# Keeping the attention queries and keys in fp32: one fp32 score matmul in place of three fp32r ones

## The chip, the cores and the metric

The kernel runs on one core of a Trainium2 chip. The metric is the device time of one execution in microseconds, the median over runs. The reference computes in fp32, and the kernel follows it on TensorE in two ways: a tensor is split into a rounded part and a remainder, both of type fp32r, and a product is three fp32r matmuls (high by high, high by low, low by high); or, in a few small places, an unsplit fp32 matmul is issued.

## The reference, cut to what matters

Three transformer blocks on a sequence of 512 positions of width 1024. The parts that the change touches are the scores of three attentions, all with head dimension 64:

```
# differential attention, 4 heads, 2 maps each
sc = einsum('bhmqd,bhmkd->bhmqk', q, k) * scale - slope * dist
p = softmax(sc);  w = p[:, :, 0] - lam * p[:, :, 1];  o = w @ v
# bidirectional retention, 4 heads: (q k^T * decay) @ v
# banded attention, 16 query heads, 4 key heads, blocks of 128, window 128
scores = einsum('bcqhgd,bckhd->bchgqk', rope(q), rope(k)) * hd ** -0.5
```

Around them stand input projections, gates, output projections, an mLSTM mixer and two feed-forward layers; they are the bulk of the matmuls.

## The kernel before

Activations lie feature-major in SBUF as eight tiles of 128x512 (XH and XL are the split, normed input). Weights stream in chunks of 1 MB into RAW (two buffers) and are split by ScalarE and VectorE into WH and WL. `mm3` (line 234) issues the three fp32r matmuls of a product; `mm` (line 226) issues one matmul of whatever type its operands have. `split` (line 247) is the pair of instructions that makes high and low parts: a copy on ScalarE (line 202), then a subtraction on VectorE (line 215).

Split activations live in FR, a pool of 25 buffers of 128x512 (`NFR`, `fr.take`, `fr.put`); unsplit ones in FT, a pool of 12. PSUM has eight banks (`bank`).

The order of the work on each engine is fixed when the program is built. Two Python generators, a main one (projections, then the output projection) and a side one (the heads), are interleaved by `weave` (line 122): each queue carries a planned time, each token a planned due time, and whichever stream is due is emitted next, the side one first when both are. A generator that yields None is blocked until the other one moves. At run time every engine follows its own list in order and waits on the others by semaphores.

Three stages matter here:

- **Block 1.** `block1_proj` projects; before each q chunk (queries and keys of one differential head) and each r chunk (retention) it waits until `len(fr.q) >= 4 + 2 * held[0]`. `qk_norm3` and the r branch split their results into FR. `diff_heads` computes the scores of 16 items (4 heads x 4 query tiles), each item two maps: map 0 contracts over partitions 0 to 63, map 1 over 64 to 127. `ret_heads` does 16 items with one score product each.
- **Banded attention.** `a_proj` projects keys (chunk 0), values (chunk 1), and queries (chunks 2 to 5, called pairs 0 to 3), with the same FR test before each q or k chunk; `rope2` rotates each of the ten tiles, with an fp32 matmul against a permutation, and splits it into FR. `a_heads` works through 32 items (pair, query block, half); stage 1 of an item is two score products over the same 64 partitions, 384 columns wide for inner query blocks and 256 wide for the first and last. Later stages do the softmax, transpose the weights, split them into FR and multiply with the values. It keeps 8 FR buffers for itself; the keys hold 4 and every query pair 4, which come free when the pair's last item is done.
- **Output projection.** `out_proj` splits each finished mixed tile into two FR buffers (`make`, `parts`), which it keeps to its end, as soon as the tile is there and FR has room. Its matmuls read FR and WH, WL.

Of the kernel before, what the change touches and what calls it, by code (L numbers as in the profile page):

```python
# [5 lines left out]
ALU = mybir.AluOpType  # L6
# [150 lines left out]
def blocks_kernel(nc, A, out):  # L157
# [16 lines left out]
    SM = sb("SM", [128, NSMALL])  # L174
    G = sb("G", [128, KT, S])
    VV = sb("VV", [128, 4 * 4 * 258], F32R)
    FR = sb("FR", [128, NFR, S], F32R)
    FT = sb("FT", [128, NFT, S])
    STR = sb("STR", [128, 896])
    ONE = sb("ONE", [128, 128])  # L180
# [53 lines left out]
    def mm3(o, L, R, start, stop, *after, last=None):  # L234

        mm(o, L[0], R[0], start, False, *after, last=False)
        mm(o, L[0], R[1], False, False, last=False)
        return mm(o, L[1], R[0], False, stop, last=last)

    def tr(o, i, ident, *after, last=True):  # L240
        f = lambda e: e.transpose(o, i, ident)  # L241
# [236 lines left out]
    def block1_proj():  # L478
        for c in B_ORDER:
            n = int(c[1])  # L480
            if c[0] == "a":
                yield from vproj("va", n)
                if n == 1:
                    small1()
                    strips()
            elif c[0] == "v":
                yield from vproj("vr", n)
            elif c[0] == "q":
                while len(fr.q) < 4 + 2 * held[0]:
                    yield None  # L490
                j, h, l, wt = w_use()
                for u in range(2):
                    yield from fm_tile(h, l, wt, u * 128)
                    b, t = st["pb"], st["pt"]
                    got = qk_norm1(b, t)
                    held[0] += 1
                    soon.append((got[3], lambda n=n, u=u, got=got: qk_step2(n, u, got)))
                w_done[j] = t
            elif c[0] == "g":
                j, h, l, wt = w_use()  # L500
                for u in range(2):
                    yield from fm_tile(h, l, wt, u * 128)
                    gate_tile(st["pb"], st["pt"], 2 * n + u, ACT.Silu)
                w_done[j] = st["pt"]
            else:
                while len(fr.q) < 4 + 2 * held[0]:
                    yield None
                j, h, l, wt = w_use()
                for u in range(2):
                    fh, f1 = fr.take()  # L510
                    fl, f2 = fr.take()
                    yield from fm_tile(h, l, wt, u * 128)
                    b, t = st["pb"], st["pt"]
                    f, ff = ft.take()
                    t1 = stt(FT[:, f, :], PS[:, b, :], 1.0 if n == 0 else 0.125, RB[:, :], ALU.mult, ALU.mult, t, st["rbt"], ff)
                    bank.put(b, t1)
                    st["rb_read"] = t1
                    tk = split(FT[:, f, :], FR[:, fh, :], FR[:, fl, :], t1, f1, f2)
                    ft.put(f, tk)
                    ready["rqk", n, u] = (fh, fl, tk)  # L520
                w_done[j] = t
        while held[0]:
            yield None
        st["xfree"] = st["pt"]
# [79 lines left out]
    def qk_norm3(x):  # L604
        f, t1, n, t, wcol = x
        b, fb = bank.take()
        t = spread(b, lambda i: FT[:, n, i * 128:(i + 1) * 128], t, fb)
        ft.put(n, t)
        w = ready["w8"][0] if wcol == C_QN else SM[:, wcol:wcol + 1]
        t = stt(FT[:, f, :], FT[:, f, :], w, PS[:, b, :], ALU.mult, ALU.mult, t, t1, ready["w8"][1], t_sm)  # L610
        bank.put(b, t)
        fh, f1 = fr.take()
        fl, f2 = fr.take()
        tk = split(FT[:, f, :], FR[:, fh, :], FR[:, fl, :], t, f1, f2)
        ft.put(f, tk)
        return fh, fl, tk

    def small1():

# [67 lines left out]
    def diff_heads():  # L687
# [10 lines left out]

        def scores(hd, qt, tb):

            (qh, ql, qt_), (kh, kl, kt_) = ready["qk", hd]
            r = []
            for m in range(2):
                b, fb = bank.take()
                p = slice(64 * m, 64 * m + 64)
                q = (FR[p, qh, qt * 128:(qt + 1) * 128], FR[p, ql, qt * 128:(qt + 1) * 128])
                t = mm3(PS[:, b, :], q, (FR[p, kh, :], FR[p, kl, :]), True, True, qt_, kt_, fb)
                st["qk_read"] = t
                s, sf = ft.take()
                nm, sm, rs = sc(), sc(), sc()  # L710
                bs = STR[:, 384 - 128 * qt:896 - 128 * qt]
                t1 = DV.op(lambda e, s=s, b=b, bs=bs, nm=nm: e.tensor_tensor_reduce(
                    out=FT[:, s, :], in0=PS[:, b, :], in1=bs, scale=1.0, scalar=-NEG,
                    op0=ALU.add, op1=ALU.min, accum_out=nm), t, tb, sf, us=0.6)
                bank.put(b, t1)
                r.append((s, sm, nm, t1, rs))
                st["bias_read"] = t1
            return r
# [25 lines left out]
        def values(hd):  # L744
            b, fb = bank.take()
            for kt in range(4):
                cc = slice(hd * 128, hd * 128 + 128)
                t = mm3(PS[:, b, :], (VT[:, 0, kt, cc], VT[:, 1, kt, cc]),
                        (FR[:, w0:w0 + 4, kt * 128:kt * 128 + 128], FR[:, w0 + 4:w0 + 8, kt * 128:kt * 128 + 128]),
                        kt == 0, kt == 3, wtok[hd], ready["va", hd // 2], fb)  # L750
            wfree[0] = ready["dpv", hd] = t
            for x in ready["qk", hd]:
                fr.put(x[0], st["qk_last", hd])
                fr.put(x[1], st["qk_last", hd])
            if hd == 3:
                for i in range(8):
                    fr.put(w0 + i, t)
            return head_norm(b, t, hd, ready["sub"])

        s1, s2 = {}, {}  # L760
        for n in range(len(items) + 3):
            if n < len(items):
                hd, qt = items[n]
                while ("qk", hd) not in ready:
                    yield None
                if qt == 0:
                    tb = bias(hd)
                yield [ready["qk", hd][0][2], ready["qk", hd][1][2]]
                s1[n] = scores(hd, qt, tb)
                if qt == 3:  # L770
                    st["qk_last", hd] = st["qk_read"]
# [55 lines left out]
    def ret_heads():  # L827
# [6 lines left out]
        for n in range(len(items) + 3):  # L834

            st["fr_kept"] = 8 - 2 * len(got) if n < len(items) else 0
            if n < len(items):
                hd, kt = items[n]
                u, p = hd // 2, slice(64 * (hd % 2), 64 * (hd % 2) + 64)
                qh, ql, qt_ = ready["rqk", 0, u]  # L840
                kh, kl, kt_ = ready["rqk", 1, u]
                if kt == 0:
                    tb = ts(STV, dp, lg[:, hd:hd + 1], ALU.mult, td, tlg, st.get("bias_read"))
                    tb = stt(STV, dn, lg[:, 4 + hd:5 + hd], STV, ALU.mult, ALU.add, tb, tlg)
# [1 line left out]
                yield [qt_, kt_]  # L846
                b, fb = bank.take()
                c = slice(kt * 128, kt * 128 + 128)
                t = mm3(PS[:, b, :], (FR[p, kh, c], FR[p, kl, c]), (FR[p, qh, :], FR[p, ql, :]), True, True, qt_, kt_, fb)
                f, ff = ft.take()  # L850
                t1 = tt(FT[:, f, :], PS[:, b, :], STR[:, 384 - 128 * kt:896 - 128 * kt], ALU.mult, t, tb, ff)
                st["bias_read"] = t1
# [5 lines left out]
                got[n] = (gh, gl, tk)  # L858
                st["fr_kept"] -= 2
                if hd % 2 and kt == 3:  # L860
                    for x in (qh, ql, kh, kl):
                        fr.put(x, t)
            k = n - 3
            if k >= 0:
# [487 lines left out]
    def rope2(x):  # L1352
# [5 lines left out]
        ta = tt(FT[:, g, :], PS[:, b, :], FT[:, si, :], ALU.mult, t2, tr_, gf)  # L1358
        bank.put(b, ta)
        tb = tt(FT[:, f, :], FT[:, f, :], FT[:, ci, :], ALU.mult, t2, tr_, t1)  # L1360
        tb = tt(FT[:, f, :], FT[:, f, :], FT[:, g, :], ALU.add, ta, tb)
        ft.put(g, tb)
        fh, f1 = fr.take()
        fl, f2 = fr.take()
        tk = split(FT[:, f, :], FR[:, fh, :], FR[:, fl, :], tb, f1, f2)
        ft.put(f, tk)
        st["rope_read"] = [ta, tb]
        return fh, fl, tk

    def a_proj():  # L1370
        V = VV[:, 0:4096].rearrange("p (a i k d) -> p a i k d", a=2, i=4, k=4)
# [59 lines left out]
    def a_heads():  # L1431
# [6 lines left out]
        def stage1(n):  # L1438
# [4 lines left out]
            W = (k1 - k0) * 128  # L1443
            mo = K_BAND + (128 if qb == 0 else 0)
            mask = CO[:, mo:mo + W]
            kh, kl, tk_ = ready["ak",][m]
            p = slice(64 * ab, 64 * ab + 64)
            hq = (2 * m + ab) * 4 + (pr % 2) * 2
            mx, nm, es, sm, dn, rd = [sc(2) for _ in range(6)]
            S_, t1 = [], []  # L1450
            for g in range(2):
                qh, ql, tq = ready["aq", pr][g]
                b, fb = bank.take()
                qq = slice(qb * 128, qb * 128 + 128)
                t = mm3(PS[:, b, 0:W], (FR[p, qh, qq], FR[p, ql, qq]),
                        (FR[p, kh, k0 * 128:k1 * 128], FR[p, kl, k0 * 128:k1 * 128]), True, True, tq, tk_, fb)
                s, sf = ft.take()
                o_, i_, a_ = FT[:, s, 0:W], PS[:, b, 0:W], mx[:, g:g + 1]
                x = DV.op(lambda e, o_=o_, i_=i_, a_=a_: e.tensor_tensor_reduce(  # L1459
# [35 lines left out]
        def stage4(n, ptok, W):  # L1495
# [19 lines left out]
            if qb == 3:  # L1515
                for g in range(2):
                    ready["mix", 2 * pr + g] = ready["mixl", 2 * pr + g]
                for y in ready["aq", pr]:
                    fr.put(y[0], st["aq_last", pr])
                    fr.put(y[1], st["aq_last", pr])  # L1520
            st["apv"] = t

        s1, s2, s3 = {}, {}, {}
        for n in range(len(items) + 3):
            if n < len(items):
                while ("aq", items[n][0]) not in ready or "av" not in ready:
                    yield None
                yield [y[2] for y in ready["aq", items[n][0]] + ready["ak",]]
                s1[n] = stage1(n)
            if n - 1 in s1:  # L1530
                s2[n - 1] = stage2(*s1.pop(n - 1))
# [7 lines left out]
            fr.put(p0 + i, st["apv"])  # L1539
        for x in ready["ak",]:  # L1540
            fr.put(x[0], st["apv"])
            fr.put(x[1], st["apv"])
        ci, si, _ = ready["rope"]
        ft.put(ci, st["rope_read"])
        ft.put(si, st["rope_read"])
# [168 lines left out]
```

How the kernel before makes its waits and increments, by code:

```python
    def play(self, eng, sems):  # L90
        for need, fn, inc in self.items:
            for k, v in need:
                eng.wait_ge(sems[k], v)
            ins = fn(eng)
            if inc:
                ins.then_inc(sems[inc[0]], inc[1])
# [1488 lines left out]
        @block.sync  # L1585
        def _(e):
            SP.play(e, sems)
            e.wait_ge(sems["out"], 16 * KT)
```

## Time and profile before

| | |
|---|---|
| median of 3 runs | 1562.91 us (1561.32 to 1566.44) |
| span of the profiled execution | 1564.8 us |
| TensorE busy | 1482.5 us, 95% |
| VectorE, ScalarE busy | 886.6 us, 57%; 597.9 us, 38% |
| mean granted TensorE clock | 0.974 |

The span runs from the first to the last instruction. No time of its own is listed for the profiled execution beside the three runs; its span lies 1.9 us above their median and 1.6 us below their highest. Times in the rows are microseconds from the start of the span; durations of a single instruction, where a column says so, are nanoseconds. PE is TensorE, DVE is VectorE, ACT is ScalarE. Matmuls are pipelined: one that is shown as 0.39 us long lets the next start 0.23 us after it.

### The profile page before, as it was taken

To read this page: it belongs to the slowest core of one execution; us is meant where nothing else is said; L and a number is where in the kernel's file an instruction comes from. 1 tells how busy PE (TensorE), PEld (TensorE's weight loads), DVE (VectorE), ACT (ScalarE), POOL (GpSimd) and SP (SyncE) were. 2 spreads that over 40 slices of the span, in tenths; PEclk is the share of its full clock that TensorE was granted. 3 is DMA by queue.
4 is the path that set the end of the run, shared out by engine and by line. 5 is a ranking of instruction groups with operands and counts; after the bars stand their busy time and mean duration, and the time that the engine had idled before them with its cause. 6 is when DMAs were issued, how large, how long until landed. Compare 5 with 4: busy or idle time off the path is not lost.

```text
span 1564.8 us, 18661 instructions
## 1 busy us (share of the span) xinstructions
PE 1482.5 (95%) x7280; PEld 1227.6 (78%) x7280; DVE 886.6 (57%) x1712; ACT 597.9 (38%) x1078; POOL 37.8 (2%) x43
## 2 busy tenths in 40 slices
PE   7999998998999689999999999988989999999997
PEld 7777785787888568888888878776768888888885
DVE  5677856666676664443344466687755544344433
ACT  5555533454444443222233233455544322222321
POOL 0011000000000000000000000000000000000000
PEclk9999997999999899999999999989999999999998
DMA  6122110131221113312322233200002222323221
GB/s 226 58 80 81 48 62 27 41 108 54 81 76 45 43 54 108 108 64 96 123 97 93 74 108 108 81 27 18 11 28 96 93 101 78 107 105 108 69 91 69
DMA packets 20903, 123.07 MB, mean 79 GB/s; under 512 B 2256, under 2 KB 2896, under 8 KB 9680
## 3 DMA queue, kind: packets, MB, share of 16 engines
q1 hardware_dynamic: 20816, 121.89, 22.6%
q8 instruction: 58, 0.95, 0.2%
q14 instruction: 29, 0.24, 0.1%
HBM read 119.78 MB, written 2.10 MB: 78 GB/s over the span
## 4 chain that ended last, share of the span: by engine, by line
PE 42%; issue 24%; DVE 7%; ACT 3%; DVEq 0%; POOLq 0%; POOL 0%; ACTq 0%
PE PS L227 41%; DVE FT L223 2%; PE PS L241 1%; DVE FR L215 1%; ACT FR L202 1%; ACT WH L202 1%; DVE WL L215 1%; ACT FT L202 1%; DVE FT L219 1%; DVE FT L215 0%; DVE SC L220 0%; DVE FT L1459 0%; DVE G L215 0%; ACT XH L202 0%; DVE XT L215 0%
## 5 line engine op out<-in xcount | busy, mean ns | idle before, releaser
L227 PE MATMUL PS<-XH,WH 128*128 128x512 f32 x1080 | 427.2, 396 | 0.0
L227 PE MATMUL PS<-XH,WL 128*128 128x512 f32 x1080 | 420.8, 390 | 0.0
L227 PE MATMUL PS<-XL,WH 128*128 128x512 f32 x1080 | 420.6, 389 | 0.0
L227 PE MATMUL PS<-FR,WH 128*128 128x512 f32 x1088 | 345.7, 399 | 18.9 <-DVE FR L215 13.2
L215 DVE TENSOR_TENSOR WL<-RAW,WH 128x1024 fp32r<-128x1024 f32 (+2 forms) x242 | 263.2, 1129 | 137.9 <-ACT WH L202 136.9
L202 ACT ACTIVATE WH<-RAW 128x1024 fp32r<-128x1024 f32 (+2 forms) x242 | 223.8, 974 | 144.0 <-PE PS L227 137.8
L227 PEld LDWEIGHTS PS<-FR,WH 128*128 128x128 f32 x1088 | 205.3, 192 | 68.7 <-issue 8.1
L227 PEld LDWEIGHTS PS<-XH,WH 128*128 128x128 f32 x1080 | 202.8, 188 | 46.8 <-issue 6.2
L227 PEld LDWEIGHTS PS<-XH,WL 128*128 128x128 f32 x1080 | 202.7, 188 | 42.8
L227 PEld LDWEIGHTS PS<-XL,WH 128*128 128x128 f32 x1080 | 202.9, 188 | 40.8 <-issue 0.7
L227 PE MATMUL PS<-FR,WL 128*128 128x512 f32 x544 | 215.3, 396 | 0.0
L202 ACT ACTIVATE FR<-FT 128x512 fp32r<-128x512 f32 (+3 forms) x118 | 69.4, 588 | 355.2 <-DVE FT L215 296.9
L215 DVE TENSOR_TENSOR FT<-PS,RB 128x512 f32<-128x512 f32 x89 | 61.0, 688 | 213.8 <-PE PS L227 200.8
L215 DVE TENSOR_TENSOR FR<-FT,FR 128x512 fp32r<-128x512 f32 (+3 forms) x118 | 75.3, 638 | 85.4 <-ACT FR L202 85.4
L227 PEld LDWEIGHTS PS<-FR,WL 128*128 128x128 f32 x544 | 104.2, 192 | 22.2
L227 PE MATMUL PS<-WH,XH 128*128 128x256 f32 x288 | 84.1, 292 | 11.4 <-DVE XL L223 11.4
L227 PE MATMUL PS<-FR 64*128 64x512 f32 (+3 forms) x384 | 85.0, 391 | 7.3 <-DVE G L215 2.9
L202 ACT ACTIVATE FT<-FT 128x512 f32<-128x512 f32 (+2 forms) x81 | 40.7, 504 | 125.0 <-DVE FT L215 100.9
L227 PE MATMUL PS<-WL,XH 128*128 128x256 f32 x288 | 82.5, 286 | 0.0
L227 PE MATMUL PS<-WH,XL 128*128 128x256 f32 x288 | 82.4, 286 | 0.0
L227 PEld LDWEIGHTS PS<-FR 64*128 64x128 f32 (+1 forms) x384 | 57.0, 200 | 30.8 <-issue 14.6
L227 PE MATMUL PS<-FR,VV 128*128 128x256 f32 (+1 forms) x336 | 65.2, 335 | 12.0 <-DVE FR L215 11.8
(110 smaller groups left out, 1331.0 us busy)
## 6 DMA issues: line engine op xcount, KB each, us to landing
RAW<-in_f_in SPq DMA_DIRECT2D x44, 1024.0 KB, 4.9
RAW<-in_w_in SPq DMA_DIRECT2D x13, 1024.0 KB, 4.9
RAW<-in_m_in SPq DMA_DIRECT2D x12, 1024.0 KB, 4.9
RAW<-in_f_oa SPq DMA_DIRECT2D x16, 768.0 KB, 4.2
RAW<-in_f_ob SPq DMA_DIRECT2D x16, 640.0 KB, 3.9
RAW<-in_a_in SPq DMA_DIRECT2D x6, 1024.0 KB, 4.9
RAW<-in_w_out SPq DMA_DIRECT2D x4, 1024.0 KB, 4.9
RAW<-in_m_out SPq DMA_DIRECT2D x4, 1024.0 KB, 4.9
```

The source lines that it names most:

```text
L202: return AC.op(lambda e: e.activation(o, i, f, scale=scale) if accum is None else e.activation(o, i, f, scale=scale, accum_out=accum), *af ...
L215: return q.op(lambda e: e.tensor_tensor(o, a, b, op), *after, us=us)
L219: return q.op(lambda e: e.tensor_scalar(o, a, s1, None, op0), *after, us=dve_us(o))
L223: return DV.op(lambda e: e.scalar_tensor_tensor(out=o, in0=a, scalar=s, in1=b, op0=op0, op1=op1), *after, us=dve_us(o))
L227: f = lambda e: e.matmul(o, l, r, start=start, stop=stop, skip_group_check=True)
L241: f = lambda e: e.transpose(o, i, ident)
```

## The change

Query and key tiles of the three attentions are no longer split. They are written once, in fp32, into FP, a second view of the memory of FR with type fp32, so that each takes one buffer of the pool and not two. Their scores are one fp32 matmul each (`mm4`), and the planner is told that it lasts as long as two fp32r matmuls of that width. All waits that asked for the split's end now ask for the one VectorE instruction that writes the tile. The FR tests ahead of the chunks stay as they are.

```diff
-    FR = sb("FR", [128, NFR, S], F32R)
+    at, _ = nc.bump_sbuf(NFR * S * 4)
+    FR = nc.alloc_sbuf_tensor_at("FR", [128, NFR, S], F32R, offset=at)
+    FP = nc.alloc_sbuf_tensor_at("FP", [128, NFR, S], F32, offset=at)
...
+    def mm4(o, l, r, start, stop, *after, last=None):
+        f = lambda e: e.matmul(o, l, r, start=start, stop=stop, skip_group_check=True)
+        us = 2 * 0.00042 * width(o)
+        if stop if last is None else last:
+            return PE.op(f, *after, us=us)
+        PE.quiet(f, *after, us=us)
+        return None
...
# block1_proj, r branch (qk_norm3 likewise)
-                    t1 = stt(FT[:, f, :], PS[:, b, :], 1.0 if n == 0 else 0.125, RB[:, :], ALU.mult, ALU.mult, t, st["rbt"], ff)
+                    t1 = stt(FP[:, f, :], PS[:, b, :], 1.0 if n == 0 else 0.125, RB[:, :], ALU.mult, ALU.mult, t, st["rbt"], ff)
-                    tk = split(FT[:, f, :], FR[:, fh, :], FR[:, fl, :], t1, f1, f2)
-                    ft.put(f, tk)
-                    ready["rqk", n, u] = (fh, fl, tk)
+                    ready["rqk", n, u] = (f, t1)
...
# rope2
-        tb = tt(FT[:, f, :], FT[:, f, :], FT[:, g, :], ALU.add, ta, tb)
+        x, xf = fr.take()
+        tb = tt(FP[:, x, :], FT[:, f, :], FT[:, g, :], ALU.add, ta, tb, xf)
-        fh, f1 = fr.take()
-        fl, f2 = fr.take()
-        tk = split(FT[:, f, :], FR[:, fh, :], FR[:, fl, :], tb, f1, f2)
...
# diff_heads; ret_heads and a_heads likewise
-                t = mm3(PS[:, b, :], q, (FR[p, kh, :], FR[p, kl, :]), True, True, qt_, kt_, fb)
+                t = mm4(PS[:, b, :], FP[p, q, qt * 128:(qt + 1) * 128], FP[p, k, :], True, True, qt_, kt_, fb)
```

## Rows read from the trace of the kernel before

**Rows 1.** The page: span, and busy time of each engine.

```profile
span 1564.8 us, 18661 instructions
...
PE 1482.5 (95%) x7280; PEld 1227.6 (78%) x7280; DVE 886.6 (57%) x1712; ACT 597.9 (38%) x1078; POOL 37.8 (2%) x43
```

**Rows 2.** Busy time in stretches (columns: length, PE, PEld, DVE, ACT, POOL, clock, DMA).

```profile
40.00:214.00 174.00, 170.66 (x916) 137.97 (x915) 123.98 (x286) 91.39 (x159) 17.11 (x12) 1.00 0.19 67
214.00:290.00 76.00, 69.54 (x324) 51.32 (x322) 46.10 (x70) 26.06 (x41) 5.15 (x4) 0.89 0.08 28
...
1026.00:1050.00 24.00, 19.76 (x101) 16.85 (x99) 19.27 (x67) 12.56 (x44) 0.00 (x0) 0.72 0.12 44
1050.00:1080.00 30.00, 30.00 (x179) 25.07 (x178) 22.88 (x88) 15.48 (x54) 0.00 (x0) 1.00 0.00 1
1080.00:1154.00 74.00, 60.05 (x341) 48.78 (x339) 53.50 (x190) 39.13 (x128) 0.00 (x0) 0.90 0.05 15
```

**Rows 3.** The same columns, for three stretches at the lower clock.

```profile
238.50:255.50 17.00, 14.39 (x35) 9.45 (x35) 11.39 (x17) 7.66 (x12) 1.38 (x1) 0.50 0.18 62
1030.50:1044.00 13.50, 11.27 (x48) 9.79 (x46) 9.12 (x36) 6.87 (x24) 0.00 (x0) 0.50 0.14 60
1088.50:1102.00 13.50, 10.00 (x33) 7.82 (x32) 8.91 (x24) 5.37 (x16) 0.00 (x0) 0.50 0.23 79
```

**Rows 4.** Waits of TensorE between 1026 and 1154 us.

```profile
PE PS L227 <- DVE FR L215: 16.3, 11, 3.5
```

**Rows 5.** Timeline: the two longest of those waits (columns: start, length, instruction, wait).

```profile
1087.60 0.95 PE L227 MATMUL PS<-FR,VV 128*128 128x256 f32 x6 [2.79 <-DVE FR L215]
...
1092.86 1.19 PE L227 MATMUL PS<-FR,WH 128*128 128x512 f32 x2 [3.50 <-DVE FR L215]
```

**Rows 6.** Timeline: fp32r matmuls of 512 columns, back to back.

```profile
145.82 0.39 PE L227 MATMUL PS<-XH,WH 128*128 128x512 f32 x1
...
146.50 0.39 PE L227 MATMUL PS<-XH,WH 128*128 128x512 f32 x1
```

**Rows 7.** Timeline: one fp32 matmul of 512 columns (two records) amid fp32r ones.

```profile
965.03 1.02 PE L227 MATMUL PS<-FT,CO 128*128 128x512 f32 x2
...
965.50 0.68 PE L227 MATMUL PS<-WH,XH 128*128 128x256 f32 x1
...
966.01 0.28 PE L227 MATMUL PS<-WL,XH 128*128 128x256 f32 x1
```

**Rows 8.** Timeline: the scores of one differential item, and what follows.

```profile
144.12 0.97 PE L227 MATMUL PS<-FR 64*128 64x512 f32 x6
...
145.02 0.50 PE L227 MATMUL PS<-XH,WH 128*128 128x512 f32 x1
```

**Rows 9.** Timeline: the first retention scores, four items in a row.

```profile
214.29 3.01 PE L227 MATMUL PS<-FR 64*128 64x512 f32 x12
```

**Rows 10.** Timeline: one banded item of 384 and one of 256 columns, and their successors.

```profile
1052.98 1.31 PE L227 MATMUL PS<-FR 64*128 64x384 f32 x6
1054.23 0.50 PE L227 MATMUL PS<-XH,WH 128*128 128x512 f32 x1
...
1072.95 0.97 PE L227 MATMUL PS<-FR 64*128 64x256 f32 x6
1073.85 0.50 PE L227 MATMUL PS<-XH,WH 128*128 128x512 f32 x1
```

**Rows 11.** Groups by shape (count | busy us, mean ns of one | idle before, releaser).

```profile
L215 DVE TENSOR_TENSOR FR<-FT,FR 128x512 fp32r<-128x512 f32 x94 | 65.1, 692 | 72.2 <-ACT FR L202 72.2
...
L202 ACT ACTIVATE FR<-FT 128x512 fp32r<-128x512 f32 x94 | 59.4, 632 | 342.1 <-DVE FT L215 296.9 <-DVE FT L223 45.2
...
L227 PE MATMUL PS<-FR 64*128 64x512 f32 x144 | 31.3, 435 | 2.9 <-DVE G L215 2.9
...
L227 PE MATMUL PS<-FR 64*128 64x384 f32 x96 | 22.8, 371 | 0.2 <-DVE FR L215 0.2
...
L227 PE MATMUL PS<-FR 64*128 64x256 f32 x96 | 16.4, 314 | 0.0
```

More of the change, by code:

```diff
@@ L509, in block1_proj @@
                 for u in range(2):
-                    fh, f1 = fr.take()
-                    fl, f2 = fr.take()
+                    f, ff = fr.take()
                     yield from fm_tile(h, l, wt, u * 128)
                     b, t = st["pb"], st["pt"]
-                    f, ff = ft.take()
-                    t1 = stt(FT[:, f, :], PS[:, b, :], 1.0 if n == 0 else 0.125, RB[:, :], ALU.mult, ALU.mult, t, st["rbt"], ff)
+                    t1 = stt(FP[:, f, :], PS[:, b, :], 1.0 if n == 0 else 0.125, RB[:, :], ALU.mult, ALU.mult, t, st["rbt"], ff)
                     bank.put(b, t1)
                     st["rb_read"] = t1
-                    tk = split(FT[:, f, :], FR[:, fh, :], FR[:, fl, :], t1, f1, f2)
-                    ft.put(f, tk)
-                    ready["rqk", n, u] = (fh, fl, tk)
+                    ready["rqk", n, u] = (f, t1)
                 w_done[j] = t
@@ L609, in qk_norm3 @@
         w = ready["w8"][0] if wcol == C_QN else SM[:, wcol:wcol + 1]
-        t = stt(FT[:, f, :], FT[:, f, :], w, PS[:, b, :], ALU.mult, ALU.mult, t, t1, ready["w8"][1], t_sm)
+        x, xf = fr.take()
+        t = stt(FP[:, x, :], FT[:, f, :], w, PS[:, b, :], ALU.mult, ALU.mult, t, t1, ready["w8"][1], t_sm, xf)
         bank.put(b, t)
[L612 to L616, printed above, removed]
+        ft.put(f, t)
+        return x, t
     def small1():
@@ L699, in scores @@
         def scores(hd, qt, tb):
-            (qh, ql, qt_), (kh, kl, kt_) = ready["qk", hd]
+            (q, qt_), (k, kt_) = ready["qk", hd]
             r = []
@@ L705, in scores @@
                 p = slice(64 * m, 64 * m + 64)
-                q = (FR[p, qh, qt * 128:(qt + 1) * 128], FR[p, ql, qt * 128:(qt + 1) * 128])
-                t = mm3(PS[:, b, :], q, (FR[p, kh, :], FR[p, kl, :]), True, True, qt_, kt_, fb)
+                t = mm4(PS[:, b, :], FP[p, q, qt * 128:(qt + 1) * 128], FP[p, k, :], True, True, qt_, kt_, fb)
                 st["qk_read"] = t
@@ L753, in values @@
                 fr.put(x[0], st["qk_last", hd])
-                fr.put(x[1], st["qk_last", hd])
             if hd == 3:
@@ L767, in diff_heads @@
                     tb = bias(hd)
-                yield [ready["qk", hd][0][2], ready["qk", hd][1][2]]
+                yield [ready["qk", hd][0][1], ready["qk", hd][1][1]]
                 s1[n] = scores(hd, qt, tb)
@@ L839, in ret_heads @@
                 u, p = hd // 2, slice(64 * (hd % 2), 64 * (hd % 2) + 64)
-                qh, ql, qt_ = ready["rqk", 0, u]
-                kh, kl, kt_ = ready["rqk", 1, u]
+                q, qt_ = ready["rqk", 0, u]
+                ky, kt_ = ready["rqk", 1, u]
                 if kt == 0:
@@ L848, in ret_heads @@
                 c = slice(kt * 128, kt * 128 + 128)
-                t = mm3(PS[:, b, :], (FR[p, kh, c], FR[p, kl, c]), (FR[p, qh, :], FR[p, ql, :]), True, True, qt_, kt_, fb)
+                t = mm4(PS[:, b, :], FP[p, ky, c], FP[p, q, :], True, True, qt_, kt_, fb)
                 f, ff = ft.take()
@@ L860, in ret_heads @@
                 if hd % 2 and kt == 3:
-                    for x in (qh, ql, kh, kl):
+                    for x in (q, ky):
                         fr.put(x, t)
@@ L1360, in rope2 @@
         tb = tt(FT[:, f, :], FT[:, f, :], FT[:, ci, :], ALU.mult, t2, tr_, t1)
-        tb = tt(FT[:, f, :], FT[:, f, :], FT[:, g, :], ALU.add, ta, tb)
+        x, xf = fr.take()
+        tb = tt(FP[:, x, :], FT[:, f, :], FT[:, g, :], ALU.add, ta, tb, xf)
         ft.put(g, tb)
-        fh, f1 = fr.take()
-        fl, f2 = fr.take()
-        tk = split(FT[:, f, :], FR[:, fh, :], FR[:, fl, :], tb, f1, f2)
-        ft.put(f, tk)
+        ft.put(f, tb)
         st["rope_read"] = [ta, tb]
-        return fh, fl, tk
+        return x, tb
     def a_proj():
@@ L1445, in stage1 @@
             mask = CO[:, mo:mo + W]
-            kh, kl, tk_ = ready["ak",][m]
+            ky, tk_ = ready["ak",][m]
             p = slice(64 * ab, 64 * ab + 64)
@@ L1451, in stage1 @@
             for g in range(2):
-                qh, ql, tq = ready["aq", pr][g]
+                q, tq = ready["aq", pr][g]
                 b, fb = bank.take()
                 qq = slice(qb * 128, qb * 128 + 128)
-                t = mm3(PS[:, b, 0:W], (FR[p, qh, qq], FR[p, ql, qq]),
-                        (FR[p, kh, k0 * 128:k1 * 128], FR[p, kl, k0 * 128:k1 * 128]), True, True, tq, tk_, fb)
+                t = mm4(PS[:, b, 0:W], FP[p, q, qq], FP[p, ky, k0 * 128:k1 * 128], True, True, tq, tk_, fb)
                 s, sf = ft.take()
@@ L1519, in stage4 @@
                     fr.put(y[0], st["aq_last", pr])
-                    fr.put(y[1], st["aq_last", pr])
             st["apv"] = t
@@ L1527, in a_heads @@
                     yield None
-                yield [y[2] for y in ready["aq", items[n][0]] + ready["ak",]]
+                yield [y[1] for y in ready["aq", items[n][0]] + ready["ak",]]
                 s1[n] = stage1(n)
@@ L1541, in a_heads @@
             fr.put(x[0], st["apv"])
-            fr.put(x[1], st["apv"])
         ci, si, _ = ready["rope"]
```

## The prediction

> **What bounds the kernel now.** I read the page first: TensorE is busy 1482.5 of 1564.8 us, VectorE 57%, ScalarE 38% [rows 1]. So work added to TensorE costs about its own length wherever TensorE has no holes, and work taken from VectorE and ScalarE pays only through a hole that it closes. Next the busy time in stretches, to see where holes are. The differential stage (40 to 214 us) has 3.3 us of them in 174; the retention stage (214 to 290) has 6.5; the banded stage has 4.2 between 1026 and 1050, none in the next 30 us, and 14.0 between 1080 and 1154 [rows 2]. The granted clock is 1.00 in the dense stretches and 0.72, 0.89 and 0.90 where the holes are. Asking for the low stretches alone shows full half-clock stretches (0.50, that is 1.2 in place of 2.4 GHz), each beginning at or just after a hole: TensorE is busy 14.39, 11.27 and 10.00 us in them [rows 3]. At the full clock that work would take about half, so they cost some 7.2, 5.6 and 5.0 us on top of the holes themselves. Then the waits: from 1026 to 1154 the waits of TensorE are put down to VectorE's FR writes, 16.3 us [rows 4], the longest 2.79 and 3.50 us [rows 5].
>
> What starves TensorE there is read from the code beside these rows. With 25 FR buffers, a_heads holds 8, the keys 4, pairs 0, 1 and 2 hold 12: one is left, and the projection of pair 3 wants 4. It is blocked until pair 0 is done, and between 1026 and 1050 the heads run with nothing to fill their latency. The same happens to the output projection: its first two mixed tiles exist once pair 0 is done, but with all pairs projected only 25-8-4-12 = 1 buffer is free until pair 1 is done; its first matmul is the one that waits 3.50 us at 1092.86 [rows 5].
>
> **What the scores cost.** The steady fp32r matmul of 512 columns: from 145.82 to 146.50 lie three starts, 0.227 us each [rows 6], 0.68 per product. An fp32 product of 512 columns exists once in kind, the rotation matmul: two records, first at 965.03; the second record behind it (WL,XH) starts normally at 966.01, and its neighbour of 256 columns takes about 0.12 of array time, so the fp32 product holds the array from 965.03 to 965.89, 0.86 us [rows 7]. One fp32 matmul is thus 0.18 us dearer than the three it replaces, with all 128 rows.
>
> *Retention*: one product per item on one half of the rows. Twelve matmuls take 3.01 us including the last one's tail, so 64-row fp32r matmuls on the same rows follow each other at the same 0.23 [rows 9]. 16 items x 0.18 = +2.9 us.
>
> *Differential*: the six matmuls of an item last 0.97 us together, and the next stream starts 0.90 after the first of them [rows 8]; in series they would need 6 x 0.227 = 1.36. So the two maps, on different halves of the rows, run side by side: three slots of 0.227 plus 0.22 at the change of shape. If fp32 matmuls pair in the same way, an item takes 0.86 + 0.22 = 1.08, +0.18, and 16 items +2.9 us. If they do not, 2 x 0.86 + 0.22 = 1.94, +1.04, +16.6 us. No row shows an fp32 pair. I take the paired value, because nothing in the 64-row fp32r rows distinguishes the maps except their rows, which stay as they are, and keep the other for the range.
>
> Here a rule of the Trainium skill speaks against the rows: "TensorE: Matmul & The Clock Gate", Part 3 (The mechanism), says that matmuls start and end strictly in program order, and only weight loads are pulled ahead. The program order is three of map 0, then three of map 1, so by that rule just one adjacent couple overlaps, and the item would take five slots, not the three that [rows 8] show; the trace does not agree. Applied to the new item it gives three half-products of 0.43 in a row in place of two, which is the in-order rival below.
>
> *Banded*: both products of an item use the same rows, so nothing pairs. Six matmuls and their change of shape take 1.25 us at 384 columns and 0.90 at 256 [rows 10]; less 0.20 that is 1.05 and 0.70. The fp32 cost scaled by width is 2 x 0.86 x 384/512 = 1.29 and 2 x 0.86 x 256/512 = 0.86: +0.24 and +0.16. The 96 matmuls of either width are 16 items [rows 11]: 3.8 + 2.6 = +6.4 us. From below, if 64-row fp32 were no dearer than its planned two slots, each product would fall from three slots to two; from above, 0.18 per product whatever its width gives 64 x 0.18 = 11.5.
>
> Scores together: 2.9 + 2.9 + 6.4 = **+12.2 us**, all on TensorE.
>
> **What the splits give.** 22 splits go (8 differential tiles, 4 retention, 10 banded), each 0.632 us of ScalarE and 0.692 of VectorE [rows 11]: 13.9 and 15.2 us. The 12 of block 1 lie behind 3.3 us of holes in 174 and are worth nothing. The 10 banded ones shorten the rotation, which shares VectorE with the softmax; they act through the holes counted next. If that cover of TensorE work were absent, a tile would be ready 1.3 us sooner, ten times; 13 us is the most they could be worth.
>
> **What the buffers give.** Banded stage after: 8 + 2 + 4 x 2 = 18, seven left. The test for 4 passes for every pair, so the 16 products of pair 3 are there at 1026 to fill the heads' latency. I count the first shortage as gone: 4.2 us of holes and 5.6 of slow clock, -9.8. The second (holes of 2.79 and 3.50, slow clock 5.0, together 11.3) comes when pair 3 is projected and VectorE is loaded with its rotation and with weight splits; the FR room removes one of its causes, but now that moment comes earlier, when pair 0 has only just delivered tiles. I take half, -5.6. The drain of the last items, the remaining 7.7 us of holes before 1154, stays, as nothing is left to fill it. Block 1: differential heads follow their q chunks there and TensorE has no holes; in the retention stage out_proj begins when the values and its first weights are ready, not when FR has room. Nothing gained in either. No DMA is added or moved past another; the weight loads follow the chunks, and pair 3's chunk asks for its successor some 20 us sooner, with the queues nearly empty then (DMA share 0.12) [rows 2].
>
> Sum: 12.2 - 9.8 - 5.6 = **-3.2 us**, from 1564.8 to 1561.6 of span. No run is listed as the profiled one; what lies around the span is at most the 1.6 us to the highest run, and the edit does not touch it. Against the median of 1562.9 the same difference gives 1559.7; I forecast 1560.
>
> **The rivals.**
>
> *Both shortages vanish.* All of 9.8 + 11.3 = 21.1 against 12.2: -8.9, 1554. For it: between 1050 and 1080, with pair 3's products as filler, there is no hole at all [rows 2]. Against: the filler is only moved, and what pair 3 fills early it cannot fill late. Chance 0.22.
>
> *The gain is spent.* Filler used before 1050 is missing between 1050 and 1080, the hole and the slow clock move there, and only the score cost is left: +12.2, 1575. For it: the planner books an fp32 product at 0.43 us per 512 columns where I measure 0.86, so it believes TensorE free some 0.4 us per product too early and hands out filler too freely; VectorE is busy 53.5 of 74 us at the end [rows 2]. It decides once the moved hole exceeds about 7 us. Slower. Chance 0.20.
>
> *fp32 pairs do not overlap.* +16.6 in place of +2.9 in the differential stage: -3.2 + 13.7 = +10.5, 1573. Decides if more than about half of the overlap is lost. Chance 0.13.
>
> *In-order pairs.* Three half-products in series: +0.43 per item, 16 x 0.43 = 6.9 over the forecast: 1567. The trace so far speaks against it, chance 0.05.
>
> *The scores are cheaper than I count*, two slots per product as planned. Then differential and retention lose 0.23 per item, 7.4 us; banded 1.05 to 0.70 and 0.70 to 0.47, 16 x 0.58 = 9.3; with the 15.4 of buffers -32, 1531. Against it speak [rows 7]. Chance 0.04.
>
> **How the numbers follow.** The forecast has 0.36, its own range 1554 to 1567 (none or all of the second shortage). About 0.3% (4.7 us) is what a measurement of this kernel can tell from no change, so 1558.2 and 1567.6 are the borders. Faster: 0.12 of the forecast, 0.22, 0.04 = 0.38. Same: 0.24 of the forecast, 0.03 of the in-order pairs, 0.03 of the spent gain = 0.30. Slower: 0.17 + 0.13 + 0.02 = 0.32. The range reaches from beneath the second case to above the spent gain: 1547 to 1579.
>
> **What would show it.** Two score records per product in place of three; an fp32 product 0.86 us of array time at 512 columns; differential items 1.08 us from first start to the next stream (1.94 refutes pairing); no XH,WH gap between 1026 and 1050 and a full clock there; the first FR,WH matmul of the last output projection well before 1092; 22 fewer FR<-FT instructions on ScalarE and on VectorE. I am wrong if the stage up to 1154 ends later than about 1153 less what block 1 adds, or if block 1 grows by more than some 6 us.

## The result and the profile after

The changed kernel takes 1572.19 us in the median of 7 runs (1565.53 to 1574.83), the kernel before 1562.91 (1561.32 to 1566.53): ratio 1.0047, 95% interval 1.0030 to 1.0064. By the ratio it is slower by some 7 us, with the interval from 5 to 10 (the two medians lie 9.3 us apart); 1560 was forecast. Run again on another chip it took 1.0040 (1.0027 to 1.0052) times the kernel before.

The page of the kernel after, against [rows 1]: TensorE is busy 8.3 us longer in a span that is 5.7 us longer, VectorE 13 and ScalarE 9 us less.

```profile
span 1570.5 us, 18371 instructions
...
PE 1490.8 (95%) x7168; PEld 1210.4 (77%) x7168; DVE 873.5 (56%) x1690; ACT 589.0 (38%) x1058; POOL 37.4 (2%) x43
```

The groups that answer to [rows 11]. The splits of this shape went from 94 to 72, the 22 that were counted; a score product is two records (96 + 64 + 64) where it was three matmuls.

```profile
L217 DVE TENSOR_TENSOR FR<-FT,FR 128x512 fp32r<-128x512 f32 x72 | 49.9, 693 | 55.6 <-ACT FR L204 55.6
L204 ACT ACTIVATE FR<-FT 128x512 fp32r<-128x512 f32 x72 | 45.5, 632 | 273.3 <-DVE FT L217 257.7 <-DVE FT L225 15.5
...
L244 PE MATMUL PS<-FP 64*128 64x512 f32 x96 | 35.6, 644 | 1.6 <-DVE FT L217 1.6
...
L244 PE MATMUL PS<-FP 64*128 64x384 f32 x64 | 28.2, 560 | 0.2
L244 PE MATMUL PS<-FP 64*128 64x256 f32 x64 | 18.5, 404 | 0.8 <-DVE FR L217 0.8
```

The timeline of one differential item, four retention items, and a banded item of each width, which answer to [rows 8 to 10]:

```profile
151.15 1.13 PE L244 MATMUL PS<-FP 64*128 64x512 f32 x4
152.21 0.50 PE L229 MATMUL PS<-XH,WH 128*128 128x512 f32 x1
...
214.45 3.70 PE L244 MATMUL PS<-FP 64*128 64x512 f32 x8
218.08 0.39 PE L229 MATMUL PS<-WH,XH 128*128 128x256 f32 x1
...
1010.66 1.55 PE L244 MATMUL PS<-FP 64*128 64x384 f32 x4
1012.15 0.50 PE L229 MATMUL PS<-XH,WH 128*128 128x512 f32 x1
...
1026.91 1.13 PE L244 MATMUL PS<-FP 64*128 64x256 f32 x4
1027.96 0.50 PE L229 MATMUL PS<-XH,WH 128*128 128x512 f32 x1
```

From first start to the next stream: differential 1.06 us where it was 0.90, so the two fp32 maps do run side by side; banded 1.49 for 1.25 and 1.05 for 0.90. Four retention items take 3.63, which is eight half-products of 0.43 and 0.2 at the change of shape; twelve fp32r matmuls of 0.227 and the same 0.2 are 2.92, so +0.18 each. Over all items 2.6 + 2.8 + 3.8 + 2.4 = 11.6 us; 12.2 was forecast.

Busy time in stretches, to be held against [rows 2]:

```profile
40.00:214.00 174.00, 172.64 (x883) 134.88 (x882) 116.22 (x274) 87.30 (x150) 17.12 (x12) 1.00 0.20 67
214.00:290.00 76.00, 71.14 (x317) 48.06 (x315) 46.01 (x70) 26.16 (x41) 4.77 (x4) 0.93 0.08 28
1026.00:1050.00 24.00, 24.00 (x124) 18.72 (x123) 16.65 (x53) 11.38 (x34) 0.00 (x0) 1.00 0.14 45
1050.00:1080.00 30.00, 25.18 (x102) 16.89 (x101) 20.87 (x68) 14.20 (x42) 0.00 (x0) 0.83 0.10 36
1080.00:1162.00 82.00, 71.73 (x379) 52.26 (x377) 58.21 (x225) 42.84 (x147) 0.00 (x0) 0.95 0.00 1
1162.00:1196.00 34.00, 31.77 (x120) 25.45 (x121) 20.79 (x27) 14.51 (x20) 0.00 (x0) 0.87 0.25 85
```

The shortage from 1026 to 1050 is gone, as forecast: 24.00 of 24.00 at the full clock. The next 30 us, which were dense, now have 4.8 us of holes and a clock of 0.83; 10.3 more stand up to the end of the heads, which comes 8 us later (1162 for 1154; 8 products more are done by then, as shown below, and at 0.68 us each they are 5.4 of these 8 us); and a new hole stands in the output projection behind them. The timeline shows the longest of the first 30 us and the one in the output projection:

```profile
1058.69 0.60 PE L252 MATMUL PS<-CO,FT 128*128 128x128 f32 x4
1063.17 1.19 PE L229 MATMUL PS<-FR,WH 128*128 128x512 f32 x2 [3.88 <-DVE FR L217]
1064.16 0.63 PE L229 MATMUL PS<-FR,WL 128*128 128x512 f32 x1
1064.71 2.93 PE L244 MATMUL PS<-FP 64*128 64x384 f32 x4
...
1183.51 0.70 PE L229 MATMUL PS<-FR,WH 128*128 128x512 f32 x2 [2.12 <-DVE WL L217]
```

At 1063.17 TensorE meets the first product of the output projection, which the kernel before met at 1092.86 [rows 5]. It waits 3.88 us for its split tile; the next item's scores, whose query and key tiles have long been there, stand behind it. The tile is late because VectorE splits a weight chunk and then the tile, and afterwards VectorE itself waits 2.11 us for the scores that TensorE was kept from:

```profile
1060.07 2.35 DVE L217 TENSOR_TENSOR WL<-RAW,WH 128x1024 fp32r<-128x1024 f32 x2
1062.34 0.69 DVE L217 TENSOR_TENSOR FR<-G,FR 128x512 fp32r<-128x512 f32 x1
...
1066.40 0.56 DVE L1459 CUSTOM_DVE_ANT_0 FT<-PS,CO 128x384 f32<-128x384 f32 x1 [2.11 <-PE PS L244]
```

A wait of this length is not new, though. The kernel before has it too, 27 us later: in a second profile of it, with a span of 1559.7 us, the first product of the output projection stands here.

```profile
1090.31 1.19 PE L227 MATMUL PS<-FR,WH 128*128 128x512 f32 x2 [3.88 <-DVE FR L215]
```

Nor has the changed kernel more idle time in all: TensorE is idle for 79.7 us of its span, where the kernel before has 82.3, and the mean granted clock is 0.979 for 0.974. So the question is not only what was lost, but why so little was gained against the added work.

The groups by shape from 996 us to the last value matmul of the heads, the kernel before and then after: 16 products of the output projection (one FR,WL matmul each) lay inside the attention, now 24 do. Two fences, one for each kernel.

```profile
L227 PE MATMUL PS<-FR,WL 128*128 128x512 f32 x16 | 6.8, 424 | 0.0
```

```profile
L229 PE MATMUL PS<-FR,WL 128*128 128x512 f32 x24 | 10.4, 433 | 0.0
```

### The profile page after: what moved, and what is told of

It is laid out like the page before. It is cut to its first block, busy times and chain, and to the rows that moved or that the text cites. A ratio compares the mean times of both kernels' runs of the same rounds, so it can differ in the third digit from the quotient of the medians.

```text
span 1570.5 us, 18371 instructions
## 1 busy us (share of the span) xinstructions
PE 1490.8 (95%) x7168; PEld 1210.4 (77%) x7168; DVE 873.5 (56%) x1690; ACT 589.0 (38%) x1058; POOL 37.4 (2%) x43
## 4 chain that ended last, share of the span: by engine, by line
PE 42%; issue 24%; DVE 7%; ACT 3%; DVEq 0%; POOLq 0%; POOL 0%; ACTq 0%
PE PS L229 38%; PE PS L244 2%; DVE FT L225 2%; PE PS L252 1%; DVE FR L217 1%; ACT FR L204 1%; DVE WL L217 1%; ACT WH L204 1%; ACT FT L204 1%; DVE FT L221 1%; DVE SC L222 0%; ACT XH L204 0%; DVE XT L217 0%; DVE G L217 0%; DVE FT L1459 0%
## 5 line engine op out<-in xcount | busy, mean ns | idle before, releaser
L204 ACT ACTIVATE FR<-FT 128x512 fp32r<-128x512 f32 (+3 forms) x96 | 55.5, 578 | 286.4 <-DVE FT L217 257.7
L217 DVE TENSOR_TENSOR FR<-FT,FR 128x512 fp32r<-128x512 f32 (+3 forms) x96 | 60.1, 626 | 69.3 <-ACT FR L204 68.4
L244 PE MATMUL PS<-FP 64*128 64x512 f32 (+2 forms) x224 | 81.2, 551 | 2.5 <-DVE FT L217 1.6
L217 POOL TENSOR_TENSOR SC<-SC,MH 128x1 f32<-128x1 f32 (+2 forms) x38 | 37.1, 976 | 1523.3 <-DVE SC L222 1238.4
```

The source lines that it names most:

```text
L204: return AC.op(lambda e: e.activation(o, i, f, scale=scale) if accum is None else e.activation(o, i, f, scale=scale, accum_out=accum), *af ...
L217: return q.op(lambda e: e.tensor_tensor(o, a, b, op), *after, us=us)
L244: f = lambda e: e.matmul(o, l, r, start=start, stop=stop, skip_group_check=True)
```

## The experiments

All ratios are to the kernel before in the same set of runs, with 95% intervals. 0.1% is 1.6 us.

**Four single edits.** My theory A was now that the array time of the scores is the loss; theory B that it hides in holes and the order is at fault.

The planner's price of an fp32 product, 1.0007 (0.9996 to 1.0018):

```diff
-        us = 2 * 0.00042 * width(o)
+        us = 4 * 0.00042 * width(o)
```

> The changed kernel with one edit: the planner books an fp32 score product at four slots of 0.00042 us per column in place of two. Theory A (the time is the array time of the scores, some 11.5 us, and TensorE has no room for it): the order changes, the sum of work does not; within 3 us of the changed kernel, 1569 to 1575. Theory B (the array time would hide in holes, and the loss is an order made with a wrong price): 1566 or less, and fewer holes between 1055 and 1150 us.

Two buffers held per unsplit tile and freed together, 0.9999 (0.9986 to 1.0012):

```diff
+    def fr_two():
+        x, xf = fr.take()
+        y, yf = fr.take()
+        twin[x] = y
+        return x, [xf, yf]
...
-        x, xf = fr.take()
+        x, xf = fr_two()
```

> The changed kernel, but every unsplit tile takes and holds two buffers of the FR pool, the second unused, so that the shortage of the kernel before is back. Theory A: the buffers only moved filler from one shortage to another; the shortage between 1026 and 1050 returns, the later ones shrink, and the time stays within 3 us of the changed kernel (1569 to 1575). Theory B1 (the early filler is what cost): 1566 or less. The prediction as recorded (buffers worth 15 us): 1580 or more.

Three fp32r matmuls per score in the same order, 1.0007 (0.9995 to 1.0019). This kernel leaves out the low parts of queries and keys, so its time alone is of use:

```diff
-    FP = nc.alloc_sbuf_tensor_at("FP", [128, NFR, S], F32, offset=at)
+    FP = nc.alloc_sbuf_tensor_at("FP", [128, NFR, S], F32R, offset=at)
...
+        g = lambda k: lambda e: e.matmul(o, l, r, start=start and k == 0, stop=stop and k == 2, skip_group_check=True)
         us = 2 * 0.00042 * width(o)
+        PE.quiet(g(0), *after, us=us)
+        PE.quiet(g(1), us=0.0)
+        f = g(2)
+        us = 0.0
```

> The changed kernel with the tiles rounded to fp32r when they are written and each score product issued as three fp32r matmuls on the same rounded operands (the low parts are left out of the scores), booked by the planner as the one fp32 matmul was, so every engine's order is that of the changed kernel. It isolates what the fp32 product costs. Theory A: 11.5 us of array time less, nearly all of it visible, 1560 to 1564. Theory B: the scores hide in holes, less than 4 us back, 1568 or more.

Banded attention as before (its hunks of the diff left out), 0.9992 (0.9981 to 1.0004):

> Block 1 as changed (differential and retention in fp32), the banded attention as before (split, three fp32r matmuls). From the two traces, block 1 ends 0.8 us later and the banded stage adds 5.6. Theory A: 1563 to 1566, a quarter or less of the loss. A rival in which block 1 carries the loss, hidden by the luck of one profile: 1568 or more.

Theory A falls in its simple form. Giving back the buffers, or the price, gave back the whole loss, though every fp32 product stayed. The third run tells what the products do cost in an unchanged order: from 1.0040 or 1.0047 to 1.0007, 5 to 6 us of 11.6; its 1566.7 us lies between the two expectations. Block 1 carries none of the loss that its interval would show.

Where the other half is, the granted clocks of these runs tell. A span with a mean clock of 0.98 has 4% of its time at the lower level, and TensorE, if it is busy, loses half of that. The mean clock is 0.9797 over the 7 runs of the changed kernel, 0.9794 when it was run again, and 0.9765 over the 12 runs with three fp32r matmuls. As an estimate, slow clock costs the first at most 32 us and the last at most 37. By this estimate the fp32 products add 10 to 11 us of their 11.6 to the rest of the span, and some 5 come back as less slow clock. The kernel before has 0.975 (35 runs, at most 39 us). With block 1 alone changed it is 0.980, at most 31 us: 7 us less than in the kernel before, which makes up for the 5.4 us of block 1's own scores. With two buffers it is 0.982, at most 29 us: 10 us less than in the kernel before, about what the scores add. Going by the 5 us above, the fp32 products are behind about half of that; the other half goes with the missing splits and the order built without them, and no run separates the two.

The run with the higher price has another thing to show, the place of the first product of the output projection:

```profile
1088.91 1.19 PE L229 MATMUL PS<-FR,WH 128*128 128x512 f32 x2 [3.87 <-ACT FT L207]
```

It is 26 us later than in the changed kernel, and it waits as long. With two buffers it comes at 1089.40. Both have TensorE idle for 75.9 us of their spans, for 79.7 in the changed kernel.

**Which use of the buffers.** Freed buffers let pair 3's projection start early (C), and let the output projection make split tiles early (D).

Pair 3 held back as before, 1.0025 (1.0010 to 1.0039), 1568 us and so again between the two expectations:

```diff
-            while len(fr.q) < 4 + 2 * held[0]:
+            while len(fr.q) < (10 if c == 5 else 4) + 2 * held[0]:
```

> The changed kernel, one number changed: the test ahead of query pair 3's projection in the banded attention asks for 10 free buffers in place of 4, so that it starts when pair 0 is done, as in the kernel before. Theory C (what the freed buffers do is to let pair 3's projection be handed out too early, and that costs some 7 us): at most 1566, with a hole at the lower clock near 1030 again and less of them from 1060 to 1110. Rival D (the harm is in the early splits of the output projection): no change from the changed kernel, 1570 or more.

The output projection's tiles held back as before, 0.9989 (0.9975 to 1.0002); `cap` starts at 0 with the heads:

```diff
-            ok = k < KT and ("mix", k) in ready and len(fr.q) >= 2 + st.get("fr_kept", 0)
+            ok = k < st.get("cap", KT) and ("mix", k) in ready and len(fr.q) >= 2 + st.get("fr_kept", 0)
...
             if qb == 3:
+                st["cap"] = (0, 2, 4, KT)[pr]
```

> The changed kernel, but during the banded attention the output projection may make its split tiles only as far as the buffers of the kernel before let it: none while pairs 0 and 1 run, 2 once pair 1 is done, 4 once pair 2 is, then all. Pair 3's projection is early, as changed. Theory C: no repair, 1570 or more (worse if the filler is missed, up to 1578). Rival D: 1566 or less.

Two buffers and the price of four slots together, 1.0007 (0.9997 to 1.0017):

> Both earlier repairs at once: two buffers held per unsplit tile, and the planner's price of four slots. Either alone gave back all of the loss. If they repair the same thing (the too early filler), together they give no more than one: 1561 to 1567. If they are separate causes of some 7 us each, 1556 to 1559.

The changed kernel again, 1.0040 (1.0027 to 1.0052):

> The changed kernel once more, on the chip of this set, as the measure for the other three: 1.003 to 1.0065 times the kernel before, as first measured, so about 1569 to 1574. If it is within 0.2% of the kernel before here, the loss was of the earlier chip and the theories have nothing to explain.

With the two-buffer run, which is of another set and holds back block 1's buffers too, these make a square:

| ratio to before | pair 3 early | pair 3 late |
|---|---|---|
| output tiles early | 1.0040 | 1.0025 |
| output tiles late | 0.9989 | 0.9999 |

The output tiles account for 0.5% in the left column and 0.3% in the right. Pair 3 early costs 0.15% together with them and gives 0.1% without them; the intervals separate neither from nothing. Theory C falls as the main cause, D stands. Price and buffers seem to repair the same thing: together they give no more than either.

In the left column, both runs of one set, the output tiles act mostly through the clock. Made early they go with a mean clock of 0.9794 (9 runs), made late with 0.9843 (11 runs), by the estimate above at most 32 us and 25 us of slow clock; of the 8 us between the two runs that leaves about 1 for everything else. The profiles agree: TensorE is idle for 79.7 and 78.8 us, and from 1026 to 1196 us the clock is 0.92 and 0.96. Why the clock is lower with early tiles, no run isolates.

The run with late tiles has this at the place of the 3.88 us wait: the scores no longer stand behind a product. The first of the item's two starts at once; the second still waits 2.77 us, so only one of the two was ready.

```profile
1056.91 0.60 PE L252 MATMUL PS<-CO,FT 128*128 128x128 f32 x4
1057.44 0.91 PE L244 MATMUL PS<-FP 64*128 64x384 f32 x2
1061.12 1.62 PE L244 MATMUL PS<-FP 64*128 64x384 f32 x2 [2.77 <-DVE FR L217]
1062.67 1.65 PE L229 MATMUL PS<-FR,VV 128*128 128x256 f32 x6
```

**The other half, a second profile, and the products kept for the drain.** Only the banded attention in fp32 (block 1's hunks left out), 1.0032 (1.0019 to 1.0046):

> Block 1 as before (split, three fp32r matmuls), only the banded attention in fp32: the other half of the earlier run. If the loss is all in the banded stage, 1569 to 1574. If block 1 gained something that hid a part of it, above 1574; if the loss needs both, 1567 or less.

The kernel before, once more, 0.9989 (0.9976 to 1.0002), its profile with a span of 1559.7 us:

> The kernel before, as a kernel of its own, for a second profile: the first one was taken on an execution 3 us above the median. Ratio 1.000 within 0.15%. If the second profile has less slow clock in the banded stage than the first (34 us), the stage of the first overstated what there was to gain.

From 1026 to 1196 us it has some 27 us at the lower clock where the first profile has 34 (the two late stretches of [rows 3] and one of 7 us from 1154), so the first profile did overstate the room.

Tiles held back further, 0.9950 (0.9933 to 0.9967); the edit is shown against the run with late tiles:

```diff
-                st["cap"] = (0, 2, 4, KT)[pr]
+                st["cap"] = (0, 2, st["cap"], KT)[pr]
...
+            if n == len(items):
+                st["cap"] = 6
```

> The changed kernel with the output projection's split tiles held back further: 2 once pair 1 is done, no more until the last scores are issued, then 6; so 8 products move from pairs 2 and 3 into the drain of the last items, which has four holes of 1.2 to 1.8 us and 6.8 us of slow clock. Theory D2 (filler is worth more in the drain than in the pairs): 5 to 9 us under the run with late parts (1562.6), 1554 to 1558. Rival (the pairs miss it as much as the drain gains): 1561 to 1566.

Late tiles and three fp32r matmuls per score, again without the low parts, 0.9953 (0.9934 to 0.9973):

> The run with late parts, and again each score product as three fp32r matmuls on rounded tiles (the low parts of queries and keys are left out), booked and ordered the same. In the changed kernel's order this took off 5.5 us of 11.5 us of array time. If more of the array time is visible where holes are fewer: 8 to 11 us off, 1552 to 1555. If the same part is hidden: 5 to 6 off, 1557.

The fp32r form takes 0.36% off here too, 5.6 us: about the same half of the array time shows in either order, and again the clock is lower with it, 0.9816 for 0.9843, at most 4 us. Holding back gave 0.4%: the drain of the last items, where late tiles left 5.8 us of holes in 20, is filled. The two stretches of 20 us, late tiles and then held back, in the columns of [rows 2]:

```profile
1139.00:1159.00 20.00, 14.24 (x64) 11.55 (x63) 6.49 (x16) 6.81 (x18) 0.00 (x0) 0.83 0.00 0
```

```profile
1140.00:1160.00 20.00, 19.78 (x100) 16.65 (x101) 10.62 (x20) 9.32 (x20) 0.00 (x0) 1.00 0.13 49
```

The timeline of the held-back run shows products between the value matmuls of the last items, where the run with late tiles waits 1.26, 1.21 and 1.81 us:

```profile
1141.89 0.70 PE L229 MATMUL PS<-FR,WH 128*128 128x512 f32 x2 [0.22 <-DVE FR L217]
...
1143.34 0.89 PE L229 MATMUL PS<-FR,VV 128*128 128x256 f32 x6
...
1144.43 0.71 PE L229 MATMUL PS<-FR,WH 128*128 128x512 f32 x2
...
1145.90 0.94 PE L229 MATMUL PS<-FR,VV 128*128 128x256 f32 x6
```

**Does that need the change?** The same holding back in the kernel before, 0.9971 (0.9960 to 0.9982), and beside it the held-back changed kernel again, 0.9951 (0.9937 to 0.9964):

> The kernel before (split queries and keys, three fp32r matmuls per score) with the same holding back: 2 split tiles of the output projection once pair 1 is done, no more until the last scores are issued, then 6. If holding back is worth 6 us whatever the scores are, 1556 to 1559, and the fp32 scores with their freed buffers are worth nothing by themselves. If the freed buffers are needed for it (in the drain the split tiles take two buffers each of a fuller pool), 1560 or more.

> The changed kernel with the holding back once more, beside the run above on the same chip: 0.995 times the kernel before, within 0.2%, 1555 to 1559.

Most of the gain is of the order, not of the change. Each of the two expectations is half right: the kernel before comes down too, but only by 0.3%. The rest, 0.2% or 3 us, is what fp32 scores, with their freed buffers and missing splits, are then worth; the intervals overlap a little, so it is likely and not certain. The held-back changed kernel, 1556 to 1557 us, is the fastest with the full computation and beats both kernels.

## Why the prediction was wrong

- **The scores' cost, +12.2 us of array time:** right, 11.6 measured, term by term. That it lies on the path in full was nearly right, but 5 to 6 us are all that the time shows: by the estimate above some 5 more are made up for by less slow clock, which the prediction did not count for the scores.
- **The fp32 pairs overlap:** right, 1.06 us per item against 1.08. The rule of the Trainium skill ("TensorE: Matmul & The Clock Gate", Part 3, The mechanism) that matmuls start strictly in program order would have given three half-products of 0.43 and the 0.2, 1.5 us; the item disagrees with it after as it did before.
- **Block 1 gives and takes nothing beside its scores:** 0.9992 with block 1 changed alone, against 0.9989 of the kernel before measured against itself, so its own 5.4 us of scores do not show either; its mean clock was 0.980 for 0.975. The clock of single executions varies there: with the same code up to there, the stretch from 214 to 290 us has a clock of 0.93, 0.98 and 0.89 in three profiles.
- **"What the buffers give", -15.4 us: the step that failed.** Of its two parts the first, pair 3 filling 1026 to 1050, happened as described, and the 9.8 us did not stay: its products were missing behind 1050, as the rival of the spent gain said, and the run with early pair 3 and late tiles waits there too, 2.77 us at 1061.12. The second part, half of 11.3 us from an earlier output projection, had the wrong sign. Measured, one buffer in place of two costs 0.4 to 0.5%, some 7 us, and holding the output projection's tiles back gives all of it back. How the early tiles cost is in part argued. An earlier product is not filler if its input is late: it is placed on TensorE ahead of work of which a part is ready. But the kernel before and the run with the higher price have such a wait of 3.9 us as well, only later. That 24 products are used for 16 leaves less for the end of the heads and for the weight splits behind them (the hole of 2.12 us at 1183.51); the run with the higher price has both, and no loss. What tells the orders apart is the place of the first product: in the profiles with fp32 scores in the banded attention it stands before 1070 us where the ratio is 1.0032 to 1.0047, and after 1088 where it is 1.0025 or less.
- **"What the splits give"** was put at nothing for block 1 and inside the holes for the banded stage. The run with late tiles and three fp32r matmuls has neither fp32 products nor these splits, and takes 0.9953. Its tiles are as late as in the kernel before, and by the square the early pair 3 gives 0.1%. So some 5 to 6 us go with the missing splits and the orders built without them; that it is the splits is not shown, as no run puts them back alone.
- **The rivals.** In time the fp32 pairs that do not overlap, 1573, came nearest, by luck: they do overlap. In kind it was the spent gain, 1575 at a chance of 0.20. It named the planner's price as the reason, and pricing the product at four slots did repair the loss: it moved the first product of the output projection from 1063 to 1089 us, as holding two buffers did. Pair 3 held back moved it to 1090.49 too and gave back less than half, so its place is not all.
- The forecast's own range, 1554 to 1567 for all or none of the second shortage, was summed wrongly: with none it is 12.2 - 9.8 = +2.4 us, 1565.
- The shortages were sized from one profile that was above the kernel's median and had more slow clock than its second one; this made the term larger, not its sign wrong.

## What to carry to other kernels

A freed buffer is not a gain where work is handed out greedily in a fixed order: ask which work becomes possible sooner, whether its own inputs are ready then, and which later hole it was filling. Filler was worth most here in the drain of the last items (0.4% for 8 products), where nothing else could run; keep some back for it, and size what a hole is worth from where its filler is taken. Price changes on the bound engine from the array time per item, which carried over to within 5% here, and look at the mean granted clock beside the time: here it made up for about half of what the items cost.

## What the runs showed of the hardware

- Two fp32 matmuls of 64 rows on different halves of the array run side by side, like fp32r ones: 1.06 us for the pair, which is the 0.86 of one and the 0.2 at the change of shape.
- An fp32 matmul costs 0.43 us per record of 512 columns and two records, on 64 rows as on 128; at 256 and 384 columns it scales with the width, while the fp32r one it replaces does not quite (0.117 us at 256 columns [rows 10], where 0.227 at 512 gives 0.114), so the narrow ones lose less: +0.075 us per product at 256 against +0.18 at 512.
- One order of instructions is executed with different stretches of slow clock: between 1026 and 1200 us the changed kernel had four in one profile and three in the other, and its runs spread over 9 us.
- With the same order, fp32 score products went with a higher mean granted clock than three fp32r matmuls each: 0.9797 and 0.9794 for 0.9765, and 0.9843 for 0.9816 with late tiles.
